# Computing the second layer's adaLN modulation in small pieces inside the first layer's convolution loop

## Chip, cores and metric

One Trainium2 chip, 8 cores. Each core runs the same program on one of the 8 sequences of the batch, without talking to the others. The metric is the device time of the slowest core in microseconds (us); the figure of a kernel is the median of its runs.

## What is computed

Two layers, each of the form x <- x + gate(c) * Mixer(RMSNorm(x) * (1 + scale(c)) + shift(c)). Layer 0 mixes with a causal depthwise convolution of width 31, layer 1 with dilated attention. Sequence length 2048, width 1024. The part that the change touches is the modulation of a layer, which depends on the conditioning vector c and on weights alone:

```
def ada_modulation(c, w, b):              # w: 1024 x 3072 for each layer
    mod = jax.nn.silu(c) @ w + b
    shift, scale, gate = jnp.split(mod, 3, axis=-1)
    return shift[:, None, :], scale[:, None, :], gate[:, None, :]

def conformer_conv_mixer(h, w_in, conv_w, conv_b, ln_g, ln_b, w_out):
    proj = h @ w_in
    val, glu_gate, z = jnp.split(proj, 3, axis=-1)
    u = val * jax.nn.sigmoid(glu_gate)
...
    u = jax.nn.silu(layer_norm(u, ln_g, ln_b))
    return (u * jax.nn.silu(z)) @ w_out
```

Between the two shown lines on u stands the depthwise convolution over time, with its bias.

## The kernel before

A small class, `Prog`, holds one list of instructions for each engine (pe, act, dve, pool, sp). `P.op` and `P.dma` put an instruction on the list of the engine that is named, in the order of the Python program, and put semaphore waits ahead of it, worked out from the names of what it reads and writes. Each engine runs its list strictly in order. A DMA that is put on "pool" is issued by GpSimd, which first sits through the DMA's waits; all later work of GpSimd stands behind it. `P.barrier()` makes every engine but TensorE wait for all that was put on any list before it.

Order of the work up to the end of the convolution:

- **Start.** SyncE loads x in 16 tiles, then the gate biases (`gate_rep<-gateb`, two for layer 0 and two for layer 1). GpSimd loads layer 0's modulation weights `ada_w` in three parts (shift, scale, gate) of 1024 x 1024, converted to bf16 (2048 KB each as stored), into two slots of the arena.
- **`phase_norm` with `emit_mod(0)`.** `emit_mod(l)` is the modulation of layer l: for each part it waits for the part's weights and multiplies. For shift and scale, silu(c) is the stationary operand and the weights stream through (L307, 16 matmuls of 512 columns), and the row that results is turned into a column (L318). For the gate, silu(c) repeated 128 times is the stationary operand (L331, 16 matmuls). Then the normalised x is transposed (L378) and scaled and shifted into `hT` (L383 on ScalarE, L388 on VectorE).
- **`emit_mod(1)`**, the same for layer 1, straight after the last transpose. Its three weight loads are issued by GpSimd, the third one when a slot is free again. Then a barrier.
- **Convolution loop of `layer0`,** 8 channel blocks cc of 128 channels. For each: `make_diag(cc+1)` (GpSimd writes 31 diagonal matrices, L472), 4 time tiles of GLU input projections (L507 and L510, 8 matmuls of 128x512 each, banks 0 to 3), the issue of loads for later (`load_w(cc+2)`, 512 KB, and `w0z`, 256 KB, which is 128 columns of a weight matrix), then 4 time tiles of convolution (L533, 31 matmuls of 128x512, banks 4 and 5). Behind each convolution tile, `stats` of the tile before it sums over channels on TensorE (L477 into bank 6, L480 into bank 7), and VectorE adds the two banks into S1 and S2 (L489). `stats` of a block's last tile comes behind the next block's first GLU tile.
- **After the loop:** the last `stats`, a barrier, the layer norm, the z projection (L602), the output projection (L639), and layer 1's norm, which is the first reader of layer 1's shift and scale. Layer 1's gate is read at the end of layer 1. The last 11264 bytes of the arena (from `TOP`) are filled by `l1_prefetch0` after that barrier and are unused until then.

All DMAs carry the line of the helper, L98.

Of the kernel before, what the change touches and what calls it, by code (L numbers as in the profile page):

```python
# [5 lines left out]
F32 = mybir.dt.float32  # L6
# [5 lines left out]
D = 1024  # L12
# [130 lines left out]
class Arena:  # L143
# [7 lines left out]
    def reset(self, off=0):  # L151
        self.off = off

    def alloc(self, shape, dtype):
        n = 1
        for s_ in shape:
            n *= s_
        esz = 4 if dtype == F32 else 2
        nb = (n * esz + 31) // 32 * 32
        o = self.off  # L160
        self.off += nb
        self.peak = max(self.peak, self.off)
        assert self.off <= getattr(self, "limit", self.nbytes), f"arena overflow {self.off} > {getattr(self, 'limit', self.nbytes)}"
        if dtype == F32:
            ap = self.t[:, o // 4: o // 4 + n]
        else:
            ap = self.tb[:, o // 2: o // 2 + n]
        if len(shape) == 2:
            return ap.rearrange("p (a b) -> p a b", a=shape[0])
        if len(shape) == 3:  # L170
            return ap.rearrange("p (a b c) -> p a b c", a=shape[0], b=shape[1])
        return ap
# [19 lines left out]
def build(layers, first, last):  # L192
# [48 lines left out]
    arena.peak = 0  # L241
    arena.limit = TOP
    l1_prefetched = []

    def l1_prefetch0():
        w1h = w1_d[0].rearrange("(c p) n -> p c n", p=128)
        P.dma("pool", "emask0", top_em0[:, :, :], emask_d[0].rearrange("p (a b) -> p a b", a=6), writes=["Em0"])
        P.dma("pool", "w1z", top_zsl[:, :, :], w1h[:, :, 1152:1280], writes=["w1z"])
        P.dma("pool", "w1s0", top_gsl0[:, :, :], w1h[:, :, 0:384], writes=["w1s0"])
        l1_prefetched.append(True)  # L250

    P.dma("pool", "cst", cst[:, :], cst_d, writes=["cst"])
# [40 lines left out]
    def emit_mod(l):  # L293
            adaw_l = adaw_d[l].rearrange("(c p) n -> p c n", p=128)
            for part in range(3):
                sl = ada_dma(l, part)
                if part == 2:
                    for half in range(2):
                        P.dma("sp", f"gbias{l}_{half}", gate_rep[:, l, half * 512:(half + 1) * 512],
                              gateb_d[0:1, l * D + half * 512:l * D + (half + 1) * 512].broadcast_to([128, 512]),  # L300
                              writes=[f"gate_rep{l}_{half}"])
                if part < 2:
                    for half in range(2):
                        def mmr(e, sl=sl, half=half):
                            r = None
                            for dc in range(8):
                                r = e.matmul(banks[1 + half][0:2, :], lhsT=sc2h[:, dc, :],  # L307
                                             rhs=adaslot[sl][:, dc, half * 512:(half + 1) * 512], start=(dc == 0), stop=(dc == 7))
                            return r
                        P.op("pe", mmr, reads=[f"adaslot{sl}", "sc2h"], writes=[BK[1 + half]])  # L310
                        P.op("act", lambda e, half=half: e.activation(out=rowb[0:1, half * 512:(half + 1) * 512],
                                                                      in_=banks[1 + half][0:1, :], func=AF.Copy),
                             reads=[BK[1 + half]], writes=[f"rowb{half}"])

                    def mm(e):
                        r = None
                        for j in range(8):
                            r = e.matmul(banks[0][:, 2 * j:2 * j + 2], lhsT=rowb[0:1, j * 128:(j + 1) * 128],  # L318
                                         rhs=ones_f[0:1, 0:2], start=True, stop=True)
                        return r  # L320
                    P.op("pe", mm, reads=["rowb0", "rowb1", "ones_f"], writes=[BK[0]])
                    P.op("dve", lambda e, l=l, part=part: e.tensor_tensor(
                        out=modT[:, l, part * 8:(part + 1) * 8], in0=banks[0][:, 0:16:2],
                        in1=vecs[:, (V_SHB, V_SCB)[part][l]:(V_SHB, V_SCB)[part][l] + 8], op=ALU.add),
                        reads=[BK[0], "vecs"], writes=[f"modT{l}_{part}"])
                else:
                    for half in range(2):
                        def mm(e, sl=sl, half=half, l=l):
                            r = None
                            for dc in range(8):  # L330
                                r = e.matmul(banks[1 + half][:, :], lhsT=screp[:, dc, :],  # L331
                                             rhs=adaslot[sl][:, dc, half * 512:(half + 1) * 512], start=(dc == 0), stop=(dc == 7))
                            return r
                        P.op("pe", mm, reads=[f"adaslot{sl}"] + [f"screp{dc}" for dc in range(8)], writes=[BK[1 + half]])
                        P.op("dve", lambda e, l=l, half=half: e.tensor_tensor(
                            out=gate_rep[:, l, half * 512:(half + 1) * 512], in0=banks[1 + half][:, :],
                            in1=gate_rep[:, l, half * 512:(half + 1) * 512], op=ALU.add),
                            reads=[BK[1 + half], f"gate_rep{l}_{half}"], writes=[f"gate_rep{l}_{half}"])
            P.op("dve", lambda e, l=l: e.scalar_tensor_tensor(
                out=modA[:, l, :], in0=modT[:, l, 8:16], scalar=1.0, in1=vecs[:, V_NG[l]:V_NG[l] + 8],  # L340
                op0=ALU.add, op1=ALU.mult), reads=[f"modT{l}_1", "vecs"], writes=[f"modA{l}"])

# [4 lines left out]
    def maybe_stop(tag):  # L347
        if stop_at == tag:
            for tt in range(NT):
                P.dma("sp", f"x{tt}", y_t[tt], xs[:, tt, :], reads=[f"x{tt}"])  # L350
            raise _Stop()
# [91 lines left out]
    def layer0():  # L443
        l = 0
        phase_norm(l, xn_setup, barrier=False, mod_first=0)
        for l2 in layers[1:]:
            emit_mod(l2)
        P.barrier()
        maybe_stop("norm")
        arena.reset()  # L450
        cTb = arena.alloc([8, S], BF16)
        S1 = arena.alloc([S], F32)
# [44 lines left out]
        for cc in range(8):  # L497
# [3 lines left out]
            for t4 in range(4):  # L501
                pa, pg = 0 + (t4 % 2), 2 + (t4 % 2)

                def mm(e, sl=sl, t4=t4, pa=pa, pg=pg):
                    r = None
                    for dc in range(8):
                        r = e.matmul(banks[pa][:, :], lhsT=wsl[sl][:, dc, 0:128], rhs=hT[:, dc, t4 * 512:(t4 + 1) * 512],  # L507
                                     start=(dc == 0), stop=(dc == 7))
                    for dc in range(8):
                        r = e.matmul(banks[pg][:, :], lhsT=wsl[sl][:, dc, 128:256], rhs=hT[:, dc, t4 * 512:(t4 + 1) * 512],  # L510
                                     start=(dc == 0), stop=(dc == 7))
                    return r
# [13 lines left out]
            for t4 in range(4):  # L526
                pc = 4 + (t4 % 2)

                def mmc(e, sl=sl, t4=t4, pc=pc):
                    r = None  # L530
                    for k in range(KW):
                        o = 2 + t4 * 512 + k
                        r = e.matmul(banks[pc][:, :], lhsT=diag[sl][:, k, :], rhs=ub[sl][:, o:o + 512],  # L533
                                     start=(k == 0), stop=(k == KW - 1))
                    return r
                ur = [f"u{sl}_{t4}"] + ([f"u{sl}_{t4 - 1}"] if t4 > 0 else [f"upad{sl}"])
                P.op("pe", mmc, reads=ur + [f"diag{sl}_{k}" for k in range(KW)], writes=[BK[pc]])
                if pend is not None:
                    stats(*pend)
                P.op("act", lambda e, cc=cc, t4=t4, pc=pc: e.activation(  # L540
                    out=cTb[:, cc, t4 * 512:(t4 + 1) * 512], in_=banks[pc][:, :], func=AF.Identity,
                    bias=vecs[:, V_CONVB + cc:V_CONVB + cc + 1], scale=1.0),
                    reads=[BK[pc], "vecs"], writes=[f"c{cc}_{t4}"])
                P.op("act", lambda e, cc=cc, t4=t4, pc=pc: e.activation(
                    out=csq[t4 % 2][:, :], in_=banks[pc][:, :], func=AF.Square,
                    bias=vecs[:, V_CONVB + cc:V_CONVB + cc + 1], scale=1.0),
                    reads=[BK[pc], "vecs"], writes=[f"csq{t4 % 2}"])
                pend = (cc, t4)
        stats(*pend)
        P.barrier()  # L550
        maybe_stop("A")
# [590 lines left out]
```

How the kernel before makes its waits and increments, by code:

```python
    def _waits(self, eng, need):  # L62
        for k, v in need.items():
            if k == ("e", "pe") and eng == "pe":
                continue
            if self.waited[eng].get(k, 0) >= v:
                continue
            self.waited[eng][k] = v
            h = self._handle(k)
            self.ops[eng].append(lambda e, h=h, v=v: e.wait_ge(h, v))
# [11 lines left out]
    def op(self, eng, fn, reads=(), writes=()):  # L82
        need = self._collect(reads, writes)
        self._waits(eng, need)
        self.cnt[eng] += 1
        s = self.sem[eng]
        self.ops[eng].append(lambda e, fn=fn, s=s: fn(e).then_inc(s, 1))
        self._update(reads, writes, (("e", eng), self.cnt[eng]))
# [1 line left out]
    def dma(self, eng, sname, out, in_, reads=(), writes=()):  # L90
        if sname not in self.dsem:
            self.dsem[sname] = self.nc.alloc_semaphore("d_" + sname)
            self.dcnt[sname] = 0
        need = self._collect(reads, writes)
        self._waits(eng, need)
        self.dcnt[sname] += 16
        h = self.dsem[sname]
        self.ops[eng].append(lambda e, h=h, out=out, in_=in_: e.dma_start(out=out, in_=in_).then_inc(h, 16))
        self._update(reads, writes, (("d", sname), self.dcnt[sname]))
```

## Time and profile before

| | |
|---|---|
| median of 3 runs | 1895.27 us (1894.18 to 1896.45) |
| the profiled execution | 1892.2 us |
| its span, first to last instruction of the slowest core (core 3) | 1890.4 us |
| spans of the eight cores | 1881.0 to 1890.4 us |
| mean granted TensorE clock of a core | 0.872 to 0.879 |
| matmul busy | 1529.3 us, 81% |
| VectorE, ScalarE, GpSimd busy | 42%, 44%, 13% |
| chain that ended last | TensorE 68%, VectorE 9%, ScalarE 7%, DMA 7%, issue 6% |

The span falls into stages by what TensorE runs. The set-up with both layers' modulation and the norm takes the first 173.9 us, the convolution loop the time from there to 515.7 us, and the rest of layer 0 and layer 1 what follows. In the views below, times are in us from the start of the span; "x" counts instructions; a bracket says how long the engine was idle before the group and what released it. A granted clock of 1.00 is 2.4 GHz, one of 0.50 is 1.2 GHz.

### The profile page before, as it was taken

What the parts mean: (1) busy time and instruction counts of PE and PEld (TensorE: products, weight loads), DVE (VectorE), ACT (ScalarE), POOL (GpSimd) and SP (SyncE); (2) the same over time, 40 slices, a digit from 0 to 9 for tenths busy, and PEclk for the clock granted to TensorE, in tenths of its full rate; (3) what the DMA queues carried; (4) which work ended last, traced back from release to release, by engine and by line L of the source; (5) the groups of instructions that cost most, each with busy time, mean ns of one, the idle gap of its engine ahead of it and who ended that gap; (6) DMA issues with size and microseconds to landing.
All of it is one profiled execution on the core that took longest, in us unless ns stands there. A gap on an engine that the chain in (4) does not pass through costs nothing.

```text
span 1890.4 us, 26612 instructions; the slowest of 8 cores (1881.0 to 1890.4 us)
## 1 busy us (share of the span) xinstructions
PE 1529.3 (81%) x8432; PEld 753.0 (40%) x8432; DVE 789.6 (42%) x1672; ACT 830.0 (44%) x1385; POOL 252.7 (13%) x391
## 2 busy tenths in 40 slices
PE   1345999999955787979879879879889799799738
PEld 0122444444422333444444444444444444444414
DVE  1020111111285542554455464455555555445543
ACT  2130111111153555556556555555566456555510
POOL 2014322222064321000000000000000000000020
PEclk9657999999987888979979989879889789799769
DMA  9654121111040002021021201201201201210033
GB/s 224 114 87 69 23 29 18 17 18 12 2 93 27 1 1 37 7 40 26 4 37 26 33 9 26 40 1 26 40 1 26 40 2 25 40 18 1 1 118 149
DMA packets 65367, 71.14 MB, mean 38 GB/s; under 512 B 18384, under 2 KB 51408, under 8 KB 65232
## 3 DMA queue, kind: packets, MB, share of 16 engines
q0 software_dynamic: 57456, 43.06, 16.4%
q1 hardware_dynamic: 7776, 26.39, 4.2%
q8 instruction: 71, 1.16, 0.3%
q14 instruction: 64, 0.52, 0.1%
HBM read 104.11 MB, written 8.39 MB: 60 GB/s over the span
## 4 chain that ended last, share of the span: by engine, by line
PE 68%; DVE 9%; ACT 7%; DMA 7%; issue 6%; POOL 2%; DVEq 0%; ACTq 0%; SPq 0%; POOLq 0%
PE bank L748 17%; PE bank L533 11%; PE bank L793 9%; DMA arena<-ada_w 6%; PE bank L960 5%; PE bank L993 5%; DVE arena L967 4%; PE bank L430 3%; PE bank L507 3%; PE bank L510 3%; PE bank L843 3%; PE bank L639 2%; PE bank L763 2%; PE bank L985 2%; ACT arena L1012 2%
## 5 line engine op out<-in xcount | busy, mean ns | idle before, releaser
L748 PE MATMUL bank<-hT,arena 128*128 128x512 bf16 x1536 | 369.0, 387 | 0.4 <-ACT hT L383 0.4
L967 DVE TENSOR_TENSOR arena<-arena 128x256 bf16<-128x256 bf16 (+1 forms) x768 | 184.4, 260 | 214.6 <-ACT arena L964 165.3
L964 ACT ACTIVATE arena<-bank 128x512 bf16<-128x512 f32 x320 | 163.5, 569 | 162.5 <-PE bank L960 134.7
L748 PEld LDWEIGHTS bank<-hT,arena 128*128 128x128 bf16 x1536 | 151.4, 99 | 182.2 <-issue 13.6
L533 PE MATMUL bank<-arena 128*128 128x512 bf16 x992 | 218.5, 379 | 0.0
L754 ACT ACTIVATE arena<-bank 128x512 bf16<-128x512 f32 x192 | 113.7, 596 | 152.7 <-PE bank L748 146.3
L993 PE MATMUL bank<-arena 128*128 128x32 bf16 (+1 forms) x1584 | 152.6, 263 | 31.9 <-DVE arena L967 31.3
L793 PE MATMUL bank<-hT,arena 128*128 128x512 bf16 x768 | 173.6, 379 | 0.0
L98 POOL DMA_DIRECT2D arena<-w x48 | 42.7, 895 | 959.7 <-PE bank L822 544.0
L781 DVE SCALAR_TENSOR_TENSOR arena<-bank,gq,arena 128x512 bf16<-128x512 f32 x96 | 95.0, 990 | 176.8 <-ACT arena L768 134.1
L533 PEld LDWEIGHTS bank<-arena 128*128 128x128 bf16 x992 | 96.2, 97 | 118.4
L993 PEld LDWEIGHTS bank<-arena 128*128 128x128 bf16 x1584 | 111.8, 120 | 60.4 <-issue 54.2
L765 ACT ACTIVATE arena<-bank,epsb 128x512 f32<-128x512 f32 x192 | 131.1, 683 | 9.8 <-PE bank L763 6.8
L781 DVE SCALAR_TENSOR_TENSOR arena<-bank,vecs_s,arena 128x512 bf16<-128x512 f32 x96 | 94.8, 988 | 85.0 <-ACT arena L768 46.7
L768 ACT ACTIVATE arena<-arena 128x512 f32<-128x512 f32 x192 | 120.9, 630 | 18.4 <-ACT arena L765 1.1
L960 PE MATMUL bank<-arena 64*128 64x256 bf16 (+1 forms) x768 | 124.0, 307 | 0.0
L985 PE MATMUL bank<-arena 128*128 128x256 bf16 x192 | 54.2, 394 | 74.8 <-DVE arena L967 43.3
L489 DVE TENSOR_TENSOR arena<-bank,arena 128x512 f32<-128x512 f32 x56 | 36.1, 686 | 183.0 <-PE bank L477 182.9
L793 PEld LDWEIGHTS bank<-hT,arena 128*128 128x128 bf16 x768 | 75.1, 98 | 90.7
L472 POOL TENSOR_SCALAR arena<-cstb,vecs_s 128x128 bf16<-128x128 bf16 x248 | 86.1, 362 | 152.5 <-PE bank L533 152.5
L540 ACT ACTIVATE arena<-bank,vecs_s 128x512 bf16<-128x512 f32 x32 | 22.0, 687 | 185.4 <-PE bank L533 185.4
L763 PE MATMUL bank<-arena,cstb 128*128 128x512 bf16 x192 | 74.1, 386 | 16.4 <-ACT arena L754 16.4
(94 smaller groups left out, 1647.0 us busy)
## 6 DMA issues: line engine op xcount, KB each, us to landing
arena<-w POOLq DMA_DIRECT2D x24, 768.0 KB, 9.5
arena<-ada_w POOLq DMA_DIRECT2D x6, 2048.0 KB, 31.4
xs<-x SPq DMA_DIRECT2D x16, 512.0 KB, 25.0
arena<-wo SPq DMA_DIRECT2D x16, 512.0 KB, 5.8
y<-xs SPq DMA_DIRECT2D x16, 512.0 KB, 2.6
arena<-w POOLq DMA_DIRECT2D x8, 512.0 KB, 6.2
arena<-w POOLq DMA_DIRECT2D x16, 256.0 KB, 6.5
arena<-emask POOLq DMA_DIRECT2D x8, 384.0 KB, 8.1
```

The source lines that it names most:

```text
L533: r = e.matmul(banks[pc][:, :], lhsT=diag[sl][:, k, :], rhs=ub[sl][:, o:o + 512], start=(k == 0), stop=(k == KW - 1))
L748: r = e.matmul(banks[pp][:, :], lhsT=gsl[sl][:, dc, j * 128:(j + 1) * 128], rhs=hT[:, dc, t4 * 512:(t4 + 1) * 512], start=(dc == 0), stop= ...
L754: P.op("act", lambda e: e.activation(out=sqx[:, :], in_=banks[pp][:, :], func=AF.Square), reads=[BK[pp]], writes=[sqn])
L763: P.op("pe", lambda e: e.matmul(banks[pn][:, :], lhsT=bdones, rhs=sqx[:, :], start=True, stop=True), reads=[sqn, "cst"], writes=[BK[pn]])
L765: P.op("act", lambda e: e.activation(out=sdt[b][:, :], in_=banks[pn][:, :], func=AF.Ln, scale=1.0 / 64, bias=epsb[:, 0:1]), reads=[BK[pn], ...
L768: P.op("act", lambda e: e.activation(out=sdt[b][:, :], in_=sdt[b][:, :], func=AF.Exp, scale=-0.5), reads=[f"sdt{b}"], writes=[f"sdt{b}"])
L781: P.op("dve", lambda e: e.scalar_tensor_tensor(out=o_ap, in0=i0_ap, scalar=gv, in1=i1_ap, op0=ALU.mult, op1=ALU.mult), reads=[BK[pp], f"sd ...
L793: r = e.matmul(banks[pp][:, :], lhsT=gsl[sl][:, dc, 256:384], rhs=hT[:, dc, t4 * 512:(t4 + 1) * 512], start=(dc == 0), stop=(dc == 7))
L960: r = e.matmul(banks[ps][:, off:off + ncol], lhsT=qk[g][1][p0:p0 + 64, kb * 128:(kb + 1) * 128], rhs=qk[g][0][p0:p0 + 64, kb * 128:kb * 12 ...
L964: P.op("act", lambda e: e.activation(out=PT[pt][:, 0:tot], in_=banks[ps][:, 0:tot], func=AF.Exp), reads=[BK[ps]], writes=[f"PT{pt}"])
L967: P.op("dve", lambda e, off=off, ncol=ncol: e.tensor_tensor(out=PT[pt][:, off:off + ncol], in0=PT[pt][:, off:off + ncol], in1=Emh[:, h * 3 ...
L993: r = e.matmul(banks[bk][:, c0:c0 + cs * (nc_ - 1) + 1:cs], lhsT=Vt[g][:, kb, 64 * h:64 * h + 128], rhs=PT[pt][:, o:o + nc_], start=(not s ...
```

## The change

`emit_mod(1)` ahead of the barrier is taken out. In its place:

- `mod1_prep`, behind the barrier: VectorE makes the bf16 forms of silu(c) again, in the unused end of the arena, and SyncE loads layer 1's two gate biases there instead of at the start.
- The 1024 x 3072 weights come in 24 pieces of 128 columns, 256 KB each as stored, into two slots in turn. Pieces 0 and 1 are loaded behind the barrier, ahead of the loop's own first loads.
- At the end of each block cc, behind its convolution, the three pieces 3cc, 3cc+1 and 3cc+2 are computed. A piece of shift or scale has the weights as stationary operand and silu(c), two columns wide, as moving operand: 8 matmuls with 2 columns. A piece of the gate has 8 matmuls with 128 columns. Pieces use bank 6 (even pc) and bank 7 (odd pc), and VectorE adds the bias out of the bank. Behind each piece pc, GpSimd's list gets the load of piece pc+2, which goes into the slot that piece pc was read from.

```diff
+    m1_slot = [arena.view(TOP, [8, 128], BF16), arena.view(TOP + 2048, [8, 128], BF16)]
+    m1_screp = arena.view(TOP + 4096, [8, 128], BF16)
+    m1_sc2h = arena.view(TOP + 6144, [8, 2], BF16)
+    M1REG = ["m1slot0", "m1slot1", "m1screp", "m1sc2h"]
...
+    def mod1_prep():
+        P.op("dve", lambda e: e.tensor_copy(out=m1_sc2h[:, :, :], in_=sc2[:, :, :]), reads=["sc2a", "sc2b"], writes=["m1sc2h"])
+        for dc in range(8):
+            P.op("dve", lambda e, dc=dc: e.tensor_scalar(out=m1_screp[:, dc, :], in0=ones_f[:, :], scalar1=sc2[:, dc, 0:1],
+                                                          scalar2=None, op0=ALU.mult),
+                 reads=["ones_f", "sc2a"], writes=["m1screp"])
+        for half in range(2):
+            P.dma("sp", f"gbias1_{half}", gate_rep[:, 1, half * 512:(half + 1) * 512],
+                  gateb_d[0:1, D + half * 512:D + (half + 1) * 512].broadcast_to([128, 512]),
+                  writes=[f"gate_rep1_{half}"])
+
+    def mod1_dma(pc):
+        sl = pc % 2
+        P.dma("pool", f"m1d{sl}", m1_slot[sl][:, :, :],
+              adaw_d[1].rearrange("(c p) n -> p c n", p=128)[:, :, pc * 128:(pc + 1) * 128], writes=[f"m1slot{sl}"])
+
+    def mod1_piece(pc):
+        l = 1
+        sl = pc % 2
+        part, j = pc // 8, pc % 8
+        pb = 6 + (pc % 2)
+        if part < 2:
+            def mm(e):
+                r = None
+                for dc in range(8):
+                    r = e.matmul(banks[pb][:, 0:2], lhsT=m1_slot[sl][:, dc, :], rhs=m1_sc2h[:, dc, :],
+                                 start=(dc == 0), stop=(dc == 7))
+                return r
+            P.op("pe", mm, reads=[f"m1slot{sl}", "m1sc2h"], writes=[BK[pb]])
...
+        else:
+            def mm(e):
+                r = None
+                for dc in range(8):
+                    r = e.matmul(banks[pb][:, 0:128], lhsT=m1_screp[:, dc, :], rhs=m1_slot[sl][:, dc, :],
+                                 start=(dc == 0), stop=(dc == 7))
+                return r
+            P.op("pe", mm, reads=[f"m1slot{sl}", "m1screp"], writes=[BK[pb]])
...
@@ -443,10 +506,13 @@
         phase_norm(l, xn_setup, barrier=False, mod_first=0)
-        for l2 in layers[1:]:
-            emit_mod(l2)
         P.barrier()
         maybe_stop("norm")
+        inter_mod = (1 in layers)
+        if inter_mod:
+            mod1_prep()
+            mod1_dma(0)
+            mod1_dma(1)
...
@@ -546,6 +612,11 @@
                 pend = (cc, t4)
+            if inter_mod:
+                for pc in range(3 * cc, 3 * cc + 3):
+                    mod1_piece(pc)
+                    if pc + 2 < 24:
+                        mod1_dma(pc + 2)
```

The loads of `l1_prefetch0` that fill the same end of the arena now also wait for `M1REG`; they stand behind the barrier that follows the loop.

## Rows read from the trace of the kernel before

**Rows 1.** Chain that ended last, start and length in us, stretch 0 to 520.
```profile
42.27 36.96 DMA arena<-ada_w
...
112.58 18.31 DMA arena<-ada_w
131.03 6.15 PE bank L307 x16
137.85 17.58 DMA arena<-ada_w
155.57 5.82 PE bank L331 x16
164.38 9.27 DMA arena<-w
173.89 3.46 PE bank L507 x8
```
**Rows 2.** Stages: length, each engine's busy time, then granted clock, DMA share, GB/s.
```profile
217.40:259.70 42.30, 42.30 (x197) 19.03 (x196) 7.82 (x12) 7.39 (x13) 12.51 (x34) 1.00 0.17 20
...
471.60:514.00 42.40, 42.40 (x197) 18.95 (x195) 7.82 (x12) 7.49 (x13) 0.00 (x0) 1.00 0.00 0
```
**Rows 3.** Instructions in order of time, VectorE: end of the norm, end of the modulation.
```profile
121.83 0.54 DVE L388 TENSOR_SCALAR hT<-bank,modA,modT 128x512 bf16<-128x512 bf16 x1 [1.06 <-PE bank L378]
...
162.16 0.16 DVE L339 SCALAR_TENSOR_TENSOR modA<-modT,vecs_s 128x8 f32<-128x8 f32 x1
```
**Rows 4.** The same view, GpSimd.
```profile
137.85 0.87 POOL L98 DMA_DIRECT2D arena<-ada_w  x1 [23.46 <-PE bank L307]
163.88 0.18 POOL L462 MEMSET arena<- 128x32 bf16 x2 [25.16 <-issue]
164.38 1.76 POOL L98 DMA_DIRECT2D arena<-w  x2 [0.31 <-issue]
```
**Rows 5.** DMA issues in flight from 165 to 166.1: KB each, median us to landing.
```profile
arena<-w POOLq DMA_DIRECT2D x2, 512.0 KB, 10.2
```
**Rows 6.** The same view of the whole span.
```profile
y<-xs SPq DMA_DIRECT2D x16, 512.0 KB, 2.6
...
arena<-w POOLq DMA_DIRECT2D x16, 256.0 KB, 6.5
...
gate_rep<-gateb SPq DMA_DIRECT2D x4, 256.0 KB, 36.0
...
cTs<-cT SPq DMA_DIRECT2D x1, 4.0 KB, 2.4
```
**Rows 7.** DMA queue from 56 to 79.4: packets, MB, share of 16 engines.
```profile
q1 hardware_dynamic: 573, 1.05, 21.2%
```
**Rows 8.** DMA issues in flight at 439.8 to 440.5, then at 440.6 to 441.6.
```profile
arena<-w POOLq DMA_DIRECT2D x1, 256.0 KB, 4.4
...
arena<-w POOLq DMA_DIRECT2D x2, 256.0 KB, 4.6
```
**Rows 9.** Instructions in order of time, TensorE, the end of the loop.
```profile
513.50 0.38 PE L477 MATMUL bank<-arena,ones_bf 128*128 128x512 bf16 x1
513.71 0.38 PE L480 MATMUL bank<-arena,ones_bf 128*128 128x512 bf16 x1
514.89 0.38 PE L477 MATMUL bank<-arena,ones_bf 128*128 128x512 bf16 x1 [0.80 <-DVE arena L489]
515.49 0.38 PE L480 MATMUL bank<-arena,ones_bf 128*128 128x512 bf16 x1 [0.22 <-DVE arena L489]
515.70 7.07 PE L602 MATMUL bank<-hT,arena 128*128 128x512 bf16 x32
```
**Rows 10.** The same view: transposes of 128 columns.
```profile
90.48 0.61 PE L378 MATMUL bank<-cstb,arena 128*128 128x128 bf16 x8 [0.80 <-ACT hT L383]
92.18 1.01 PE L378 MATMUL bank<-cstb,arena 128*128 128x128 bf16 x8 [1.09 <-ACT hT L383]
```
**Rows 11.** The same view: matmul groups behind idle time.
```profile
550.47 9.78 PE L602 MATMUL bank<-hT,arena 128*128 128x512 bf16 x32 [8.58 <-ACT arena L606]
...
610.40 8.84 PE L602 MATMUL bank<-hT,arena 128*128 128x512 bf16 x32 [5.49 <-ACT arena L606]
...
655.58 8.44 PE L602 MATMUL bank<-hT,arena 128*128 128x512 bf16 x32 [8.10 <-ACT arena L606]
```
**Rows 12.** The same view: two gaps under 3 us.
```profile
524.48 5.34 PE L602 MATMUL bank<-hT,arena 128*128 128x512 bf16 x24 [1.71 <-ACT arena L606]
...
862.26 0.38 PE L763 MATMUL bank<-arena,cstb 128*128 128x512 bf16 x1 [2.32 <-ACT arena L754]
862.47 2.91 PE L748 MATMUL bank<-hT,arena 128*128 128x512 bf16 x8
```

More of the change, by code:

```diff
@@ L152, in reset, with view @@
         self.off = off
+    def view(self, off, shape, dtype):
+        n = 1
+        for s_ in shape:
+            n *= s_
+        ap = self.t[:, off // 4: off // 4 + n] if dtype == F32 else self.tb[:, off // 2: off // 2 + n]
+        if len(shape) == 2:
+            return ap.rearrange("p (a b) -> p a b", a=shape[0])
+        return ap
     def alloc(self, shape, dtype):
@@ L247, in l1_prefetch0 @@
         P.dma("pool", "emask0", top_em0[:, :, :], emask_d[0].rearrange("p (a b) -> p a b", a=6), writes=["Em0"])
-        P.dma("pool", "w1z", top_zsl[:, :, :], w1h[:, :, 1152:1280], writes=["w1z"])
-        P.dma("pool", "w1s0", top_gsl0[:, :, :], w1h[:, :, 0:384], writes=["w1s0"])
+        P.dma("pool", "w1z", top_zsl[:, :, :], w1h[:, :, 1152:1280], writes=["w1z"] + M1REG)
+        P.dma("pool", "w1s0", top_gsl0[:, :, :], w1h[:, :, 0:384], writes=["w1s0"] + M1REG)
         l1_prefetched.append(True)
@@ L339, in emit_mod @@
             P.op("dve", lambda e, l=l: e.scalar_tensor_tensor(
+                out=modA[:, l, :], in0=modT[:, l, 8:16], scalar=1.0, in1=vecs[:, V_NG[l]:V_NG[l] + 8],
+                op0=ALU.add, op1=ALU.mult), reads=[f"modT{l}_1", "vecs"], writes=[f"modA{l}"])
+    def mod1_prep():
[8 more added lines that the diff above has]
+                  writes=[f"gate_rep1_{half}"])
@@ new lines, in mod1_dma @@
+    def mod1_dma(pc):
[15 more added lines that the diff above has]
+            P.op("pe", mm, reads=[f"m1slot{sl}", "m1sc2h"], writes=[BK[pb]])
+            bcol = (V_SHB, V_SCB)[part][l] + j
+            P.op("dve", lambda e: e.tensor_tensor(out=modT[:, l, part * 8 + j:part * 8 + j + 1], in0=banks[pb][:, 0:1],
+                                                  in1=vecs[:, bcol:bcol + 1], op=ALU.add),
+                 reads=[BK[pb], "vecs"], writes=[f"modT{l}_{part}"])
+        else:
[6 more added lines that the diff above has]
+            P.op("pe", mm, reads=[f"m1slot{sl}", "m1screp"], writes=[BK[pb]])
+            half = j // 4
+            P.op("dve", lambda e: e.tensor_tensor(out=gate_rep[:, l, j * 128:(j + 1) * 128], in0=banks[pb][:, 0:128],
+                                                  in1=gate_rep[:, l, j * 128:(j + 1) * 128], op=ALU.add),
+                 reads=[BK[pb], f"gate_rep{l}_{half}"], writes=[f"gate_rep{l}_{half}"])
+        if pc == 15:
+            P.op("dve", lambda e: e.scalar_tensor_tensor(
```

## The prediction

> **What bounds the kernel now.** I read the chain that ended last first, because the change moves work from one stage into another and only the chain says what each stage waits for. Before the convolution loop the chain is a row of DMA waits: layer 0's modulation weights, then layer 1's (18.31 and 17.58 us), each followed by a burst of matmuls, then the loop's first weights, 9.27 us [rows 1]. TensorE does little there. From 173.89 us on the chain is TensorE alone, and the second view, busy time by stage, says how full it is: a block of the loop lasts 42.3 to 42.4 us, TensorE is busy for all of it, at a granted clock of 1.00, and VectorE, ScalarE and GpSimd are each busy for less than a third [rows 2]. So time that the change takes out before the loop is gained whole, and every us that TensorE stands or works longer in the loop is paid whole. I then looked at what one small load costs from issue to landing, and at what TensorE's matmuls cost after it stood idle.
>
> **What is removed.** The norm ends at 121.83 + 0.54 = 122.37 us, and layer 1's modulation at 162.32 [rows 3]. GpSimd comes out of the barrier 1.56 us later (163.88) and issues the first weight load at 164.38 [rows 4]; it lands 9.27 us later, and the first GLU matmul starts at 173.89 [rows 1]. From norm to loop it is 51.5 us.
>
> **What stands there afterwards.** The barrier, 1.56 us as before. Then GpSimd's list holds the loads of pieces 0 and 1, two issues at 0.88 us (half of the 1.76 us for two), then the memsets, then the loop's own two loads: the first GLU load is issued about 2.3 us behind the barrier. It landed in 9.27 us with one other load of 512 KB beside it. That pair landed at 173.65 and, by the median of 10.2 for the two [rows 5], about 176.4, which is 12.0 us from the first issue for 1 MB. The pair of 256 KB landed 5.7 us after its first issue [rows 8]. So 512 KB more cost between 4 us (the slope in lightly loaded stretches) and 8.8 (that of the first pair against the small one), if all share; if they go in order, next to nothing but the late issue. Two gate biases of 256 KB now come here too, by SyncE. For the landing I take 14.5 us from the end of the barrier (11.6, the old landing behind a later issue, to 20). The first GLU matmul then starts at 122.37 + 1.56 + 14.5 + 0.24 = 138.7, 35.2 us earlier (30 to 38). The 9 VectorE instructions of `mod1_prep` are needed only at the end of block 0 and nobody waits for them.
>
> The two gate biases leave the start. There the four biases landed 36.0 us after their issue, in the median [rows 6], beside layer 0's last weights, which the chain waits for until 79 us [rows 1]. From 56 to 79.4 us the queue of SyncE took 21.2% of the engines for 1.05 MB [rows 7], so 0.5 MB are about 2.4 us of all engines. I take 2.0 us gained (0 to 2.4). Sum of the start: 37 us gained (30 to 40).
>
> **What is added: three pieces at the end of each block.** The order in the lists decides here. Piece 3cc+2 lies in the slot of piece 3cc, and its load stands behind piece 3cc: GpSimd can issue it only when TensorE has read that slot, in the same burst. Two pieces per burst are there beforehand, the third is loaded while TensorE waits. TensorE has nothing else, since the next block's GLU stands behind the pieces on its list. Nothing hides this; TensorE has no spare time in the loop [rows 2]. The steps, from the moment at which the next GLU would have started:
>
> 1. The piece's bank is still being read: `stats` has just written banks 6 and 7 and VectorE has to add them. The end of the loop shows the same wait: after L480 at 513.71 TensorE could go on at 513.93, bank 6 is free at 514.89 (0.96) and bank 7 at 515.49 (1.56) [rows 9]. Even blocks begin with bank 6, odd ones with bank 7: 1.26 on average.
> 2. Piece 3cc: 8 matmuls. The nearest row is 8 transposes of 128 columns, 0.61 us at the high clock, 1.01 at the low one [rows 10]. Two columns instead of 128 may be quicker; the 128x128 weight loads stay. 0.61 (0.3 to 0.65).
> 3. From TensorE's last matmul to GpSimd's issue: 131.03 + 6.15 = 137.18 to 137.85, so 0.67 [rows 1, 4].
> 4. Issue to landing. A load of 128 columns of a weight matrix, 256 KB, is of the kind of `w0z`. The 16 of this size took 6.5 us in the median, most of them behind a larger load [rows 6]; the pair at 439.84, with nothing beside it, 4.4 for the first and 4.6 in the median for both [rows 8]. Our case is that pair: 4.5 (4.4 to 6.5). The difference is that the rows read are 12 KB apart and not 1.5 KB, which no row bounds.
> 5. Landing to matmul 0.24 [rows 1], and piece 3cc+2, partly at the low clock, 0.8.
>
> That makes 1.26 + 0.61 + 0.67 + 4.5 + 0.24 + 0.8 = 8.1 us. Piece 3cc+1 lies inside step 3 and 4. GpSimd's `make_diag` for the block after next starts about 9 us later and has the whole block of 42 us for 10.8 us of work; it costs nothing.
>
> Then the clock. 32 matmuls of 512 columns take 7.07 us at 1.00 [rows 9]. The same 32 after idle times of 8.58, 5.49 and 8.10 us take 9.78, 8.84 and 8.44 [rows 11]: 2.7, 1.8 and 1.4 more, since the first ones run at 1.2 GHz. After 2.32 us idle, 8 matmuls still lose 1.0 (2.91 against 1.89), after 1.71 us nothing is lost [rows 12]. Here TensorE stands for some 5 us with three small bursts around it. I take 2.0 us (1.4 to 2.7). The Trainium skill, "TensorE: Matmul & The Clock Gate", section "HAM oscillation", says the same of short matmul bursts separated by DMA waits: each burst begins at the low clock. By that rule, the trace agrees.
>
> Per block 10.1 us, for eight blocks 81 us (70 to 92). The eighth has its stall in front of the last `stats`, on which the barrier hangs, so it counts too.
>
> **Sum.** Loop +80.8, start -37.2: +43.6 us. On the profiled execution of 1892.2 us that is 1935.8; it lies 3.1 below the median of 1895.3, so the median becomes 1939. My own range for this case: +30 (70 - 40) to +62 (92 - 30), 1925 to 1957.
>
> **The rivals.**
>
> - *Loads land slower.* All eight cores send their small loads at about the same moment, 512-byte reads out of wide rows. At 6.5 us each, the median of the loaded case [rows 6], it is 2.0 more per block, 16 in all: 1955; at the 9.27 of the loop's first load [rows 1], 1977. For it: the unknown of step 4. Against it: eight cores did the pair of rows 8 side by side as well.
> - *The clock stays up.* The small bursts count as activity enough: 16 us less, 1923. For it: the 1.71 us gap of rows 12. Against it: rows 11.
> - *Loads land sooner.* 512 KB by SyncE's queue took 2.6 us [rows 6]; at that, 1.9 less per block, 15 in all: 1924. Against it: another queue and no conversion of the data. The Trainium skill, "DMA: Bandwidth & Descriptors", section "Anatomy of one DMA", gives 2.0 us plus the bytes at 436 GB/s, 2.6 us for 256 KB, an estimate that leads to the same 1924. The trace disagrees, with 4.4 for the same amount.
> - *Faster than before.* The third piece does not stall TensorE because its weights are there. Then a block costs 1.26 + 3 x 0.61 = 3.1, the loop 25, and the total is 1895.3 - 37.2 + 25 = 1883. The point that decides is 37.2 / 8 = 4.65 us per block. Steps 1, 2, 3 and 5 alone make 3.6, so landing and clock together would have to cost under 1.1 us, while the quickest landing of the whole trace, 4 KB, is 2.4 [rows 6]. It would need a load issued before the burst, which the order of the lists excludes.
> - *No difference.* The second and the third rival together with 40 us saved at the start give 1905; some more would have to go right.
>
> **How the numbers follow.** Forecast 0.64, slower landing 0.15, clock up 0.10, quicker landing 0.05, faster 0.04, the last 0.02. The predicted time is the forecast's, 1939. The range goes from 1918, which takes in clock and quick landing, to 1962, which takes in the nearer half of slow landing. A measurement of this kernel tells about 0.2% from no change; faster 0.04, within 0.2% 0.02, slower 0.94.
>
> **What the new profile would show.** The first GLU matmul at 137 to 141 us (start right). Blocks of 52 to 53 us and not 42.3. In the order of time, at each block's end, two groups of 8 small matmuls, then TensorE idle for some 4.5 to 5 us with DMA of ada_w as the releaser, one more group, and GLU matmuls of which the first 8 or so run at 0.43 us each. GpSimd's issue about 0.7 us behind the first piece, and landings of 4.4 to 4.8 us. I am wrong if that idle time is missing (the order of the lists misread), if landings are off 4.5 us (eight times their difference), or if the granted clock after the stall is 1.00.

## The result

The changed kernel takes 1931.05 us in the median (1929.06 to 2038.12, 9 runs), the kernel before 1896.23 (1893.72 to 1975.53, 10 runs). The ratio is 1.0186, with a 95% interval of 1.0175 to 1.0197: 35 us slower, where 44 were forecast and 1918 to 1962 was the range. The profiled execution took 1931.65 us, 39.4 more than that of before; before's was 4 us below its own median. Single executions of either kernel take some per cent longer, at a lower granted clock on one die, and the ratio leaves them out.

The page of the changed kernel:

```profile
span 1929.8 us, 26940 instructions; the slowest of 8 cores (1914.3 to 1929.8 us)
...
PE 1540.2 (80%) x8544; PEld 761.0 (39%) x8544; DVE 793.7 (41%) x1701; ACT 827.5 (43%) x1381; POOL 270.0 (14%) x412
...
PE 68%; DVE 8%; DMA 7%; ACT 7%; issue 6%; POOL 2%; DVEq 0%; ACTq 0%; SPq 0%; POOLq 0%
...
arena<-ada_w POOLq DMA_DIRECT2D x3, 2048.0 KB, 33.9
arena<-ada_w POOLq DMA_DIRECT2D x24, 256.0 KB, 4.9
```

On the whole it looks like before. The difference shows in the order of time. The chain that ended last, start and length in us, core 0, against rows 1:

```profile
43.51 31.93 DMA arena<-ada_w
...
121.80 10.83 DMA arena<-w
132.77 3.57 PE bank L573 x8
...
170.06 6.71 PE bank L599 x31
178.82 5.87 DMA arena<-ada_w
185.28 3.44 PE bank L573 x8
188.72 1.80 PE bank L576 x8
```

The two long loads of 18 us are gone and the first GLU matmul starts at 132.77 us and not at 173.89. But between the last convolution tile of block 0 and block 1's first GLU matmul a load of `ada_w` stands on the chain. It comes back seven times. The same place in the order of instructions on TensorE, then on GpSimd (core 0):

```profile
176.81 0.38 PE L546 MATMUL bank<-arena,ones_bf 128*128 128x512 bf16 x1
177.92 0.34 PE L381 MATMUL bank<-arena 128*128 128x2 bf16 x8 [0.73 <-DVE arena L551]
178.52 0.34 PE L381 MATMUL bank<-arena 128*128 128x2 bf16 x8 [0.26 <-DVE modT L386]
184.93 0.36 PE L381 MATMUL bank<-arena 128*128 128x2 bf16 x8 [6.07 <-DMA arena<-ada_w]
185.14 3.57 PE L573 MATMUL bank<-hT,arena 128*128 128x512 bf16 x8
188.51 2.01 PE L576 MATMUL bank<-hT,arena 128*128 128x512 bf16 x8
```
```profile
178.82 1.75 POOL L98 DMA_DIRECT2D arena<-ada_w  x2 [26.10 <-PE bank L381]
185.94 0.88 POOL L98 DMA_DIRECT2D arena<-ada_w  x1 [5.37 <-PE bank L381]
```

Two pieces, a wait for the bank (0.73 us idle), then 6.07 us of idle time until the third piece's weights are there, issued at 178.82 when the first piece had been read. Then 8 GLU matmuls take 3.57 us, where 8 such matmuls at 2.4 GHz take 1.89: the granted clock from 185.14 to 188.70 us is 0.50. A block in the view by stage:

```profile
185.28:237.24 51.96, 45.03 (x222) 20.13 (x220) 8.30 (x15) 7.44 (x12) 15.20 (x36) 0.93 0.30 31
```

51.96 us and a granted clock of 0.93, against 42.30 us and 1.00 [rows 2].

To account for the whole, each core's span is cut at its first GLU matmul and at its first z matmul. Medians over the eight cores, in us, for every profile taken (the start is the time of the first GLU matmul):

| kernel | start | loop | behind the loop |
|---|---|---|---|
| before | 170.1 (167.1 to 173.9) | 341.9 | 1374.7 |
| changed | 131.8 (130.0 to 133.0) | 413.6 | 1379.5 |
| before, second profile | 167.4 | 342.2 | 1374.5 |
| changed, second profile | 129.9 | 412.9 | 1379.4 |
| before, third profile | 168.0 | 342.2 | 1374.0 |
| three slots | 133.0 | 363.2 | 1384.3 |
| spread | 129.6 | 349.4 | 1382.6 |
| stall filled with matmuls | 129.5 | 401.1 | 1378.0 |
| biases late | 166.5 | 342.4 | 1373.4 |
| spread, late first loads | 128.0 | 349.2 | 1380.4 |
| the same again | 127.8 | 349.0 | 1374.9 |
| without layer 1's modulation | 128.1 | 342.6 | 1384.3 |
| the same again | 127.9 | 342.2 | 1380.3 |

The change is -38.4 at the start, +71.7 in the loop and +4.9 behind it. On the slowest cores (3 before, 0 after) it is -41.1, +75.0 and +5.4.

### The profile page after: what moved, and what is told of

It reads as the page before. It is cut to its first block, busy times and chain, and to the rows that moved or that the text cites. A ratio compares the mean times of both kernels' runs of the same rounds, so it can differ in the third digit from the quotient of the medians.

```text
span 1929.8 us, 26940 instructions; the slowest of 8 cores (1914.3 to 1929.8 us)
## 1 busy us (share of the span) xinstructions
PE 1540.2 (80%) x8544; PEld 761.0 (39%) x8544; DVE 793.7 (41%) x1701; ACT 827.5 (43%) x1381; POOL 270.0 (14%) x412
## 4 chain that ended last, share of the span: by engine, by line
PE 68%; DVE 8%; DMA 7%; ACT 7%; issue 6%; POOL 2%; DVEq 0%; ACTq 0%; SPq 0%; POOLq 0%
PE bank L819 16%; PE bank L599 11%; PE bank L864 8%; DMA arena<-ada_w 5%; PE bank L1031 5%; PE bank L1064 5%; PE bank L573 4%; DVE arena L1038 3%; PE bank L576 3%; PE bank L493 3%; PE bank L914 3%; PE bank L710 2%; PE bank L834 2%; PE bank L1056 2%; ACT arena L1083 2%
## 5 line engine op out<-in xcount | busy, mean ns | idle before, releaser
L819 PE MATMUL bank<-hT,arena 128*128 128x512 bf16 x1536 | 369.1, 387 | 0.4 <-ACT hT L446 0.4
L1064 PE MATMUL bank<-arena 128*128 128x32 bf16 (+1 forms) x1584 | 158.2, 269 | 29.7 <-DVE arena L1038 29.4
L864 PE MATMUL bank<-hT,arena 128*128 128x512 bf16 x768 | 173.6, 379 | 0.0
L599 PEld LDWEIGHTS bank<-arena 128*128 128x128 bf16 x992 | 96.2, 97 | 118.4
L1064 PEld LDWEIGHTS bank<-arena 128*128 128x128 bf16 x1584 | 116.6, 123 | 58.4 <-issue 51.7
L673 PE MATMUL bank<-hT,arena 128*128 128x512 bf16 x256 | 67.3, 426 | 26.5 <-ACT arena L677 26.5
L1031 PEld LDWEIGHTS bank<-arena 64*128 64x128 bf16 x768 | 66.5, 112 | 52.8 <-issue 38.6
```

The lines of the kernel that those rows point to most:

```text
L819: r = e.matmul(banks[pp][:, :], lhsT=gsl[sl][:, dc, j * 128:(j + 1) * 128], rhs=hT[:, dc, t4 * 512:(t4 + 1) * 512], start=(dc == 0), stop= ...
L864: r = e.matmul(banks[pp][:, :], lhsT=gsl[sl][:, dc, 256:384], rhs=hT[:, dc, t4 * 512:(t4 + 1) * 512], start=(dc == 0), stop=(dc == 7))
L1031: r = e.matmul(banks[ps][:, off:off + ncol], lhsT=qk[g][1][p0:p0 + 64, kb * 128:(kb + 1) * 128], rhs=qk[g][0][p0:p0 + 64, kb * 128:kb * 12 ...
L1064: r = e.matmul(banks[bk][:, c0:c0 + cs * (nc_ - 1) + 1:cs], lhsT=Vt[g][:, kb, 64 * h:64 * h + 128], rhs=PT[pt][:, o:o + nc_], start=(not s ...
```

## The experiments

The theory was A: the third piece of each block stalls TensorE because its load can be issued only inside the burst. Its rivals were that the pieces themselves and their bank handovers cost the time, or that 24 more loads disturb the loop's own.

**A third slot.** All three pieces of a block can be loaded during the block before.

```diff
-    m1_slot = [arena.view(TOP, [8, 128], BF16), arena.view(TOP + 2048, [8, 128], BF16)]
+    m1_slot = [arena.view(TOP + 2048 * i, [8, 128], BF16) for i in range(3)]
...
-        P.dma("pool", "emask0", top_em0[:, :, :], emask_d[0].rearrange("p (a b) -> p a b", a=6), writes=["Em0"])
+        P.dma("pool", "emask0", top_em0[:, :, :], emask_d[0].rearrange("p (a b) -> p a b", a=6), writes=["Em0"] + M1REG)
...
-                    if pc + 2 < 24:
-                        mod1_dma(pc + 2)
+                    if pc + 3 < 24:
+                        mod1_dma(pc + 3)
```

> The changed kernel with a third slot, so that all three pieces of a block are loaded during the block before and none waits for a load issued in the burst. Theory A (the third piece's load, issued inside the burst, is what a block pays for): TensorE's 5 to 6 us of idle time per block goes and with it the low clock; what stays is the bank handover (1.3 us) and three small pieces with a handover between the first and the third, about 2.5 us per block instead of 9.7. Total 1931 - 8 x 7.2 = about 1873. Rival B (the pieces' own matmuls and the bank handovers cost most of the 9.7): about 1920 or more. Rival C (the small loads disturb the loop's own loads): no change, 1931.

Measured: ratio to before 0.9963 (0.9937 to 0.9989), about 1889 on the scale of 1896. The order on TensorE at the end of block 0, core 4:

```profile
180.26 0.34 PE L381 MATMUL bank<-arena 128*128 128x2 bf16 x8 [0.73 <-DVE arena L552]
180.85 0.57 PE L381 MATMUL bank<-arena 128*128 128x2 bf16 x16 [0.26 <-DVE modT L386]
181.29 1.89 PE L574 MATMUL bank<-hT,arena 128*128 128x512 bf16 x8
```

The 6.07 us of idle time are gone, the waits for the banks are there as before, and the GLU matmuls run at full speed (1.89). Of the loop's 72 added us 50 are gone: per block (363.2 - 341.9) / 8 = 2.7 are left, where 2.5 were expected. So theory A holds and both rivals fall, for the loop. The total is 16 us above what was expected. 7 are the loop's, since the changed kernel's had grown by 72 us and the expectation took 77. 5 lie behind the loop, through the edit of the line on `emask0` (below), and 1 at the start. The rest is the slowest cores': on cores 4 to 7 the loop took 365 to 370 us, against 361 on the others, which is a clock matter of its own, told at the end.

**The pieces spread over the block.** Two slots, one piece ahead of each of the last three convolution tiles, in banks 0 and 1.

```diff
-        pb = 6 + (pc % 2)
+        pb = pc % 2
...
+                if inter_mod and t4 > 0:
+                    mod1_piece(3 * cc + t4 - 1)
+                    if 3 * cc + t4 + 1 < 24:
+                        mod1_dma(3 * cc + t4 + 1)
                 ur = [f"u{sl}_{t4}"] + ([f"u{sl}_{t4 - 1}"] if t4 > 0 else [f"upad{sl}"])
```

> Two slots as in the changed kernel, but one piece ahead of each of the last three convolution tiles of a block and not three at its end, in banks 0 and 1, which are free there. Each load has at least 7 us of convolution over it. Theory A: neither a wait for a load nor one for a bank is left; 16 pieces of 2 columns at 0.2 us and 8 of 128 columns at 0.5 us make 7 us for the whole loop instead of 77. Total 1931 - 70 = about 1861. Rival B (the pieces' own work is dear): per block 5 or more, 1895 or more. It should beat the three-slot version by the bank handovers, about 10 us.

Measured: ratio 0.9826 (0.9779 to 0.9873), about 1863. TensorE in block 0, core 0:

```profile
165.83 0.38 PE L543 MATMUL bank<-arena,ones_bf 128*128 128x512 bf16 x1
166.05 0.38 PE L546 MATMUL bank<-arena,ones_bf 128*128 128x512 bf16 x1
166.26 0.34 PE L381 MATMUL bank<-arena 128*128 128x2 bf16 x8
166.47 6.87 PE L599 MATMUL bank<-arena 128*128 128x512 bf16 x30
```

No bracket, so no idle time. A piece with 2 columns occupies TensorE for 0.21 us (166.26 to 166.47). The loop is 7.5 us longer than before, as expected. The total is 26 us below that of the three slots, where 10 were expected; 14 of them are the loop's. The same 24 pieces and 24 loads that cost 72 us at a block's end with two slots cost 7.5 here: their place is the price.

**The stall filled with matmuls.** 24 matmuls of 512 columns between the second and the third piece; their result goes to bank 0 and isn't used.

```diff
+                    if pc == 3 * cc + 2:
+                        def fill(e):
+                            r = None
+                            for i in range(24):
+                                r = e.matmul(banks[0][:, :], lhsT=ones_bf[:, :], rhs=hT[:, 0, 0:512], start=True, stop=True)
+                            return r
+                        P.op("pe", fill, reads=["ones_bf", "hT0_0"], writes=[BK[0]])
                     mod1_piece(pc)
```

> The changed kernel with 24 added matmuls of 512 columns (5.2 us at 2.4 GHz) into bank 0 between a block's second and third piece, whose result nobody reads. They lie inside the wait for the load. Theory A (clock): the idle time makes the next GLU matmuls start at 1.2 GHz, which costs 1.3 to 1.8 us per block; with TensorE kept busy they run at 2.4 GHz, so 8 x 1.5 = 12 us less, about 1919. Rival: the low clock comes from the sparse pieces ahead of the wait, the filling matmuls run at 1.2 GHz themselves for 3 us, end after the load has landed, and nothing or less than 4 us is gained, or some is lost: 1927 to 1945.

Measured: ratio 1.0091 (1.0049 to 1.0133), about 1913.5 on the scale of 1896, so 18 us less than the changed kernel with more work in it. Core 5:

```profile
179.10 0.34 PE L381 MATMUL bank<-arena 128*128 128x2 bf16 x8 [0.26 <-DVE modT L386]
179.30 5.34 PE L621 MATMUL bank<-hT,ones_bf 128*128 128x512 bf16 x24
184.47 0.34 PE L381 MATMUL bank<-arena 128*128 128x2 bf16 x8
184.68 1.89 PE L573 MATMUL bank<-hT,arena 128*128 128x512 bf16 x8
```

The next GLU matmul starts 7.1 us after the last `stats` (177.61), hardly sooner than without filling (7.5 in the mean), and the filling ran at 2.4 GHz: the granted clock from 179.30 to 184.60 us is 1.00. The 8 GLU matmuls take 1.89 us. The loop is 12.5 us shorter, 1.6 per block. That is the clock's part, measured by itself: the idle time of the load's wait lowers the clock, and the sparse pieces ahead of it don't. The rest of the 18 us lies in the comparison's interval, which is 8 us to either side.

**The gate biases alone.** The kernel before, with layer 1's two biases loaded when the norm has ended (`reads=["hT7_3"]` on their loads).

> The kernel before with one part of the change alone: layer 1's two gate biases are loaded when the norm has ended and not at the start. The changed kernel shows the gate matmuls of layer 0 start at 74.4 to 75.6 us on all cores instead of 78.5 to 80.1. Theory A (the 512 KB of biases delayed layer 0's last weights): here they start at about 75 too, everything behind moves up by 4 us, and the total falls by 4 us, a ratio of 0.998. The prediction took 2.0 us. Rival: the earlier start in the changed kernel has another cause (layer 1's three weight loads are not in the queue): no shift here, ratio 1.000.

Measured: ratio 0.9999 (0.9990 to 1.0008). The chain of this kernel (core 3), then that of the kernel before in its second profile (core 4):

```profile
41.03 33.04 DMA arena<-ada_w
74.21 6.30 PE bank L332 x16
...
107.39 19.96 DMA arena<-ada_w
...
133.46 18.75 DMA arena<-ada_w
```
```profile
40.80 36.16 DMA arena<-ada_w
77.47 5.86 PE bank L331 x15
...
110.20 18.18 DMA arena<-ada_w
...
135.34 17.39 DMA arena<-ada_w
```

Theory A is right about the start: layer 0's last weights land 3.1 us sooner after their issue (33.04 against 36.16), and layer 0's gate matmuls start 3.3 us sooner. It is wrong about the total. Layer 1's weights then take 1.8 and 1.4 us longer, together as much as was gained. That the biases' bytes now stand in front of these loads fits this, but no run shows it by itself.

**Without layer 1's modulation.** Its matmuls and weight loads are left out; scale, shift and gate are the biases alone.

> Layer 1's modulation is left out altogether (its scale and shift are the biases alone, its gate the bias): no weight loads for it and no matmuls. It gives the floor for any placement. Expected: the loop at 42.4 us per block as in the kernel before, so 77 us less than the changed kernel; the loop's first weights about 3 us sooner, since no pieces are loaded ahead of them; and the 3.5 us that the z projection takes longer in the changed kernel (151.4 instead of 147.9) gone. 1931 - 77 - 3 - 3.5 = about 1847. If the rest of the program still takes 4 to 5 us longer than before on most cores, that is not from the pieces but from where the start puts the cores.

Measured: ratio 0.9791 (0.9753 to 0.9828), a median of 1860.98. Start and loop are as expected, 128.1 and 342.6. Yet the total is 14 us above the expected 1847: 6 of them since the changed kernel's loop was only 72 us longer than before, and not 77, and 8 behind the loop, which took 1384 us where 1376 was expected. To see whether the chip was the reason, it ran again beside a profile of the kernel before, and the spread version with it.

> Layer 1's modulation is left out altogether, as once before, now with a profile of the kernel before on the same chip. There it came to 1861 us where 1847 was expected, since what follows the loop took 1383 to 1390 us on its cores. Theory A (the chip of that run had a slower layer 1): here 1370 to 1380 us after the loop, 1850 us or less in all, ratio to before about 0.977. Theory B (with the start shortened, layer 1 has more of its matmuls at the lower clock): again 1380 or more after the loop on most cores, ratio 0.98 or more.

> The unchanged kernel before, for the profile beside the other two. Theory A of the run without modulation: its cores take 1370 to 1378 us after the loop, as many as that run's. Theory B: 5 to 10 us less than that run's.

Measured: ratio 0.9822 (0.9803 to 0.9842), 1858.15. Behind the loop 1380.3 in the median (1371 to 1385 by core, four of them at 1380 or more), the kernel before 1374.0 (1369 to 1378). Compared with the first profile 4 us are gone, and on the chip of that one the kernel before takes 5 us longer too, in the mean over its cores (1890 against 1885), so that part was the chip's. The last section has a clock level that only its profiles show. But 6 us are still given back behind the loop, with no piece in the program, and that isn't the chip.

Theory B puts it down to the clock. The traces show another cause beside it, in the kernel's own text. In `l1_prefetch0`, two loads now name the same regions as written:

```
P.dma("pool", "w1z", top_zsl[:, :, :], w1h[:, :, 1152:1280], writes=["w1z"] + M1REG)
P.dma("pool", "w1s0", top_gsl0[:, :, :], w1h[:, :, 0:384], writes=["w1s0"] + M1REG)
```

So the second waits for the landing of the first, though they write different bytes, and GpSimd waits with it, ahead of its multiplications for the z stage. With three slots the load of `emask` names `M1REG` too, and there are two such waits. GpSimd behind the loop, first the kernel before (core 3), then the changed one (core 0), then three slots (core 4):

```profile
518.52 1.76 POOL L98 DMA_DIRECT2D arena<-w  x2
525.74 2.85 POOL L621 TENSOR_TENSOR arena<-arena 128x512 bf16<-128x512 f32 x2 [5.46 <-ACT arena L613]
```
```profile
552.63 0.90 POOL L98 DMA_DIRECT2D arena<-w  x1
561.24 0.87 POOL L98 DMA_DIRECT2D arena<-w  x1 [7.70 <-ACT arena L684]
562.12 2.27 POOL L692 TENSOR_TENSOR arena<-arena 128x512 bf16<-128x512 f32 x2
```
```profile
511.08 0.89 POOL L98 DMA_DIRECT2D arena<-w  x1 [8.24 <-DMA arena<-emask]
516.00 0.87 POOL L98 DMA_DIRECT2D arena<-w  x1 [4.03 <-DMA arena<-w]
```

The bracket of the changed kernel names ScalarE, but the issue comes 0.64 us after the landing of the load before it, on all eight cores of both its profiles, as in the three-slot version, where the bracket names the load. Here is what lies behind the loop, cut at layer 1's first matmul, in us. Three columns are medians over the cores: from the first z matmul to GpSimd's first multiplication, from the first z matmul to layer 1, and layer 1. The last is for how long the granted clock is 0.50 in layer 1, as the mean of the cores:

| kernel | first multiplication | rest of layer 0 | layer 1 | of it at 0.50 |
|---|---|---|---|---|
| before, three profiles | 10.0 each | 208.9, 208.9, 209.0 | 1165.6, 1165.6, 1165.7 | 289, 292, 293 |
| biases late | 10.0 | 208.9 | 1164.7 | 292 |
| changed, two profiles | 12.2 each | 210.3, 210.3 | 1169.1, 1169.0 | 302, 301 |
| stall filled with matmuls | 11.9 | 209.4 | 1168.8 | 303 |
| spread, late first loads, two profiles | 12.9, 12.8 | 210.4, 210.3 | 1168.7, 1164.2 | 304, 301 |
| without layer 1's modulation, two profiles | 13.1, 12.7 | 212.4, 211.0 | 1172.6, 1169.2 | 310, 303 |
| spread | 12.9 | 210.5 | 1171.1 | 304 |
| three slots | 16.6 | 215.1 | 1169.5 | 305 |

In the changed kernel the rest of layer 0 is 1.4 us longer, and 6.2 with two such waits. So that part follows a dependency written too wide, though no run has the change without it, and the two profiles without modulation are longer still for a reason that isn't known. Layer 1's code is unchanged, and it is 3.4 us longer in both profiles of the changed kernel. Its time at the low clock is 289 to 293 us in the four profiles with the long start and without the wait, and 301 to 310 in the nine others. So theory B's clock is there as well, but it isn't all that sets the length: one profile has 301 us of it and 1164.2 in layer 1. Whether the earlier start or the wait moves it is open, since every kernel with the one has the other.

**The spread version with late first loads.** Pieces 0 and 1 are loaded behind the loop's own first loads and the first diagonal matrices.

```diff
-            mod1_dma(0)
-            mod1_dma(1)
...
         make_diag(0)
+        if inter_mod:
+            mod1_dma(0)
+            mod1_dma(1)
```

> The spread version (one piece ahead of each of the last three convolution tiles, two slots) with the loads of pieces 0 and 1 behind the loop's own first loads and the first diagonal matrices. In the changed kernel GpSimd issued three loads and was then held 5.83 us until the first of them landed, before it could issue the fourth. Theory A: without pieces ahead, the loop's first weights land as in the run without layer 1's modulation, 2 us sooner; first GLU at 126 to 129 us instead of 128 to 131.6; ratio to before 0.981 to 0.983. Rival (the gate biases on SyncE's queue delay them): no difference to the spread version.

> The spread version with the late first loads once more, beside the version without layer 1's modulation on one chip. Its loop took 348.6 to 349.7 us against 341.7 to 343.0 there. Expected: 7 us above it, all of it in the loop, and 28 to 32 us below the kernel before (ratio 0.983 to 0.985). If the two come out equal, the 7 us are given back behind the loop.

Measured: ratio 0.9842 (0.9824 to 0.9860) and, again, 0.9837 (0.9808 to 0.9865); 1861.79 and 1861.35. The first GLU matmul is at 128.0 and 127.8, as without any modulation, and 1.6 us sooner than in the plain spread version. The first loads are no longer held up. GpSimd in the changed kernel (core 0), then here (core 3):

```profile
119.83 1.86 POOL L98 DMA_DIRECT2D arena<-ada_w  x2 [11.81 <-DVE arena L359]
121.68 0.21 POOL L528 MEMSET arena<- 128x32 bf16 x2
121.80 0.90 POOL L98 DMA_DIRECT2D arena<-w  x1
128.53 0.88 POOL L98 DMA_DIRECT2D arena<-w  x1 [5.83 <-issue]
```
```profile
118.38 1.82 POOL L98 DMA_DIRECT2D arena<-w  x2 [0.50 <-issue]
120.22 10.88 POOL L536 TENSOR_SCALAR arena<-cstb,vecs_s 128x128 bf16<-128x128 bf16 x31
```

In the total the two spread versions can't be told apart. Against the version without modulation beside it the loop is 7 us longer, as expected, yet the totals differ by 3 us only, since this version took 5 us less behind the loop. It also took 5 us less there than in its own first profile (1374.9 against 1380.4), all of it in layer 1, so what one profile shows behind the loop can be off by that much.

**The two kernels again.** Both kernels as they were, profiled once more on one chip.

> The unchanged kernel before, for a profile beside the others on this chip. What follows the loop (from the first z matmul to the end of the span) takes 1369 to 1376 us on its cores in the first profile, and 1383 to 1390 us in the run without layer 1's modulation. Theory A (the start shifts the cores, and layer 1 then has more of its matmuls at the lower clock): this profile shows 1369 to 1376 again. Rival B (it is the chip): 1380 or more here too.

> The unchanged changed kernel, for a profile on the same chip. Loop 411 to 417 us, first GLU at 130 to 133 us. After the loop: by theory A of the other control 1374 to 1382 as in the first profile, by rival B some 8 us more.

The profiled executions took 1893.22 and 1926.55 us. The second lines of the first table repeat the first within 3 us at the start, 1 in the loop and 0.2 behind it: 1374.5 and 1379.4. The 5 us behind the loop are there in both profiles of the changed kernel and in none of the three of the kernel before. Rival B isn't tested by it, since this is not the chip of the first run without modulation.

## Why the prediction was right, and where its sizes were off

- **What bounds the kernel.** Right. In the loop nothing covered TensorE's stall; the loop grew by the whole of it.
- **Start: 37 us gained forecast, 38.4 in the median, 41.1 on the slowest cores.** The first GLU matmul at 137 to 141 us was forecast, and it came at 130 to 133. Two terms were off, and a figure in the working of the second doesn't follow: 12.0 us for 1 MB and 5.7 for 0.5 MB make 6.3 us for 512 KB more, not 8.8. The biases gave 4 us of earlier gate matmuls (78.5 to 80.1 became 74.4 to 75.6) where I took 2.0. And the first weights landed after 10.83 us, while I had let all four loads share; the fourth wasn't even issued, as GpSimd was held until the first had landed. Not foreseen at all: the cores used to enter the loop 6.8 us apart and now do 3.0 apart, so the slowest gained most.
- **Step 1, the bank: 1.26 forecast, 1.19 measured** (mean of 64 block ends, 8 cores of the first profile; 0.88 in even blocks, 1.49 in odd ones).
- **Steps 2 and 3, first piece and GpSimd's issue: 1.28 forecast, 1.03 measured.** The pieces of 2 columns take 0.21 us and not 0.61; the transposes of 128 columns were too dear a row for them.
- **Steps 4 and 5, load to third piece 4.74 forecast, 4.77 measured** (4.35 to 6.84), from issue to the third piece's start; the row of the pair at 439.84 was the right one, and the rows' pitch of 12 KB cost nothing that shows in the median. The third piece itself 0.55 where 0.8 was taken.
- **Sum of the stall: 8.1 forecast, 7.54 measured** (6.63 to 8.83).
- **Clock: 2.0 forecast.** The loop grew by 71.7 / 8 = 9.0 per block, which leaves 1.4 for the clock; with the stall filled, 1.6 came back. TensorE's idle time in front of the third piece was 4.9 us in the mean (4.4 to 6.8). Of the three rows that gave 1.4 to 2.7, two stood behind more than 8 us, and the one behind 5.49 us gave 1.8, so they don't order by idle time; I took their middle. The Trainium skill, "TensorE: Matmul & The Clock Gate", section "HAM oscillation", says that bursts separated by load waits each start slow. The filled stall is the test of it: the trace agrees, with 3.57 us for 8 matmuls without and 1.89 with filling.
- **Behind the loop: nothing forecast, 4.9 us measured.** This step was missing. I treated the rest of the program as fixed when its start moves, and overlooked that the change adds a wait to it: 1.4 us are in the rest of layer 0, where two loads of `l1_prefetch0` now go one after the other, and 3.4 in layer 1, which is at the low clock for longer, for a reason that is open.
- **The total.** The loop was forecast at 81 and measured at 71.7, and the forgotten 4.9 made up for half of that. That the total came within 8 us is in part luck; that the loop's stall outweighs the gained start is not.

Of the rivals, the clock that stays up and the quicker landing are out by these rows; the price of the latter, 2.6 us, came from the row of a store (`y<-xs`) and not of a load. The slower landing is out too: the load that TensorE waits for took 4.4 us in the median of the 64 block ends (4.1 to 6.6), and the 24 loads of the slowest core 4.9. The Trainium skill's estimate of 2.6 us for such a load, from "DMA: Bandwidth & Descriptors", section "Anatomy of one DMA", stays 1.5 us below the quickest of these 24 (4.1). The faster outcome needed the loads issued ahead of the burst; the third slot and the spread version are kernels in which they are, and both are faster than before.

## What to carry over

When work is moved from a stage that waits into a stage that is full, count how many buffers a burst of it uses against how many there are: the first item beyond that pays a whole load latency, at the place where nothing covers it, and the clock's recovery after it. One item between two long groups of matmuls, with its load a group ahead, costs only its own matmuls: here 7.5 us for the loop where the burst cost 72. Time taken out of a start is not all kept, so judge a change by the parts of the span (start, loop, rest) on all cores, and look for waits that its own dependencies add far behind it: two loads that name one region among what they write go one after the other.

## What was not expected of the hardware

- **GpSimd is held at the fourth load.** With three loads of 1024 rows on the way, the issue of the fourth waited 5.83 us, until the first had landed (issued at 119.83, 8.4 us to landing). On every core of both profiles of the changed kernel it comes 0.31 us after that landing, and with three slots the fifth comes 0.31 us after the second has landed. No core of any profile here has more than three of GpSimd's loads on the way. Whether it is their number that counts or that of their rows, no run varies.
- **A third clock level.** On cores 4 to 7, which are one die, four profiles have stretches at a granted clock of 0.81: three slots, spread, filled, and the first without modulation. All four are from one chip, and the nine others have none. In the loop it is 20 to 34 us with three slots and 85 us on cores 4 and 5 of the spread version, whose loop took 364 us and not 349. The chain of the three-slot version (core 4) has both:

```profile
142.77 1.73 PE bank L577 x8
...
279.99 2.10 PE bank L577 x8
```

8 matmuls in 2.10 and not 1.73 us is 0.82 of full speed, at a granted clock of 0.81. The Trainium skill, "TensorE: Matmul & The Clock Gate", Part 1, names a limit on peak current that takes a die to 13/16 (0.81) once three of its cores run dense matmuls. The row agrees with the size. But most of the loop in all profiles, with eight cores in dense matmuls, ran at a granted clock of 1.00, and it isn't settled what sets it off.
